# Residue token order, inputs laid out before the launch, four cache places and a two-pass norm in a hybrid attention, convolution and mixture-of-experts layer

## The reference

```python
z = x @ w_in + b_in                      # 5376 columns: q, k, v (12 heads of 64), ua, ub (512 each), two gates (1024 each)
q, k = partial_rotary(q, k, pos)         # first 16 of the 64 dims of a head
# attention: 3 groups of 4 heads, (window, dilation) = (128, 1), (512, 4), (2048, 16);
# query t reads keys t, t-d, t-2d, ...; the groups are merged by softmax over their log-sum-exp
A = attn @ w_attn_out                    # 256 -> 1024
u = ua * sigmoid(ub)
C = silu(LN(causal_depthwise(u, 31 taps))) @ w_conv_out + b_conv_out
h = LN(alpha * x + (sigmoid(gA) * A + sigmoid(gC) * C) @ w_o)
# experts: best of 4 groups, then the 2 best of its 8 SwiGLU experts, gates by softmax
out = LN(alpha * h + moe(h))
```

## Time and profile before

| Engine | busy, us | share of the span |
|---|---|---|
| PE, matmuls | 1188.2 | 92% |
| PE, weight loads | 946.9 | 73% |
| DVE | 842.6 | 65% |
| ACT | 583.2 | 45% |
| POOL | 287.1 | 22% |

### The profile page before, as it was taken

One profiled execution on the slowest core, in us unless ns is written; L12 is line 12 of the kernel. 1 busy time (PEld: TensorE's weight loads), 2 busy tenths in 40 slices (PEclk: granted clock), 3 DMA queues, 4 the chain that ended last, 5 costly groups with the idle time before them and its releaser, 6 DMA issues.

```text
span 1290.2 us, 16384 instructions
## 1 busy us (share of the span) xinstructions
PE 1188.2 (92%) x6098; PEld 946.9 (73%) x6098; DVE 842.6 (65%) x958; ACT 583.2 (45%) x534; POOL 287.1 (22%) x227
## 2 busy tenths in 40 slices
PE   5999999979989999979849999999999999999980
PEld 4899998868878787867536777777777777777760
DVE  1259999611220356444367999888888888888866
ACT  1222221011030224301136877777777777778750
POOL 0144340111012000320021233322333223332110
PEclk8999999978766999988959999999999999999995
DMA  7277733254013042302357999999999999999833
GB/s 224 66 257 278 286 105 111 80 172 153 5 61 119 33 184 109 105 3 100 124 238 285 365 374 368 369 357 357 360 357 363 360 355 364 356 368 367 324 85 141
DMA packets 61201, 293.09 MB, mean 227 GB/s; under 512 B 11492, under 2 KB 36766, under 8 KB 48364
## 3 DMA queue, kind: packets, MB, share of 16 engines
q1 hardware_dynamic: 45149, 262.53, 54.3%
q0 software_dynamic: 12256, 25.98, 6.8%
q10 hardware_dynamic: 3758, 4.06, 1.0%
HBM read 286.83 MB, written 41.12 MB: 254 GB/s over the span
## 4 chain that ended last, share of the span: by engine, by line
PE 87%; DVE 5%; DMA 2%; issue 2%; POOL 1%; ACT 1%; SPq 1%; POOLq 0%; ACTq 0%; DVEq 0%
PE ps L604 10%; PE ps L913 9%; PE ps L915 9%; PE ps L914 9%; PE ps L937 5%; PE ps L939 5%; PE ps L938 5%; PE ps L554 3%; PE ps L556 3%; PE ps L555 3%; PE ps L552 2%; PE ps L755 2%; PE ps L831 2%; PE ps L896 2%; PE ps L799 2%
## 5 line engine op out<-in xcount | busy, mean ns | idle before, releaser
L1623 DVE TENSOR_TENSOR region_b_split<-region_b,z_split 128x2048 fp32r<-128x2048 f32 x96 | 216.9, 2286 | 25.7 <-ACT z_split L1160 25.6
L1623 DVE TENSOR_TENSOR region_a_split<-region_a,z_split 128x2048 fp32r<-128x2048 f32 x96 | 216.7, 2285 | 23.2 <-ACT z_split L1160 23.1
L913 PE MATMUL ps<-z_split,scratch_split 128*96 128x512 f32 x512 | 206.4, 403 | 1.9 <-DVE scratch_split L1628 1.9
L915 PE MATMUL ps<-z_split,scratch_split 128*96 128x512 f32 x512 | 201.8, 394 | 0.0
L1160 ACT CAST z_split<-region_a 128x2048 fp32r<-128x2048 f32 x96 | 179.8, 1908 | 0.0
L1160 ACT CAST z_split<-region_b 128x2048 fp32r<-128x2048 f32 x94 | 176.1, 1908 | 2.0 <-PE ps L915 2.0
L604 PE MATMUL ps<-x_columns,region_b 128*128 128x272 f32 x512 | 149.5, 446 | 7.0 <-DMA region_b<-in_w_in 7.0
L1305 DVE SCALAR_TENSOR_TENSOR z_conv_gates<-scratch,column_vectors,z_conv_gates 128x512 f32<-128x512 f32 (+1 forms) x240 | 133.9, 632 | 0.0
L604 PEld LDWEIGHTS ps<-x_columns,region_b 128*128 128x128 f32 x512 | 107.5, 217 | 30.5 <-DMA region_b<-in_w_in 7.1
L913 PEld LDWEIGHTS ps<-z_split,scratch_split 128*96 128x96 f32 x512 | 85.2, 166 | 33.7 <-DVE scratch_split L1628 2.2
L915 PEld LDWEIGHTS ps<-z_split,scratch_split 128*96 128x96 f32 x512 | 83.1, 162 | 36.5
(11 more groups left out here) (280 smaller groups left out, 1985.4 us busy)
## 6 DMA issues: line engine op xcount, KB each, us to landing
region_b<-in_w_expert_gate SPq DMA_DIRECT2D x16, 2048.0 KB, 14.1
region_a<-in_w_expert_up SPq DMA_DIRECT2D x16, 2048.0 KB, 14.9
region_a<-in_w_expert_gate SPq DMA_DIRECT2D x16, 2048.0 KB, 14.0
region_a<-in_w_expert_down SPq DMA_DIRECT2D x16, 2048.0 KB, 14.6
region_b<-in_w_expert_up SPq DMA_DIRECT2D x16, 2048.0 KB, 15.3
region_b<-in_w_expert_down SPq DMA_DIRECT2D x16, 2048.0 KB, 15.0
region_b<-in_w_in SPq DMA_DIRECT2D x21, 1024.0 KB, 5.3
region_b<-in_cache_kv_w POOLq DMA_DIRECT2D x16, 512.0 KB, 3.9
```

Source lines behind the costliest of these rows:

```text
L913: pe.matmul(out, xh[:, k, :], hi[:, k, :], start=k == 0, stop=False)
L915: last = pe.matmul(out, xl[:, k, :], hi[:, k, :], start=False, stop=k == KD - 1)
L1623: ve.tensor_tensor(low_part[place][:, part], raw[place][:, part], high_part[high or w][:, part].bitcast(F32), ALU.subtract).then_inc(low_s ...
```

## The change

The change has these parts:

1. **Residue order.** The prompt's tokens stand in the order 0, 4, 8, ..., 508, 1, 5, ... in every column tile. The queries and keys of a residue are 128 neighbouring columns. Rotary tables, masks, the rows of x and y are permuted to match. The convolution keeps the order of time: `u` is written back to it (4 DVE instructions in place of 1), and the centring after it returns to residue order (9 in place of 2).
2. **x laid out outside the launch.** x comes as columns, in two halves of 128 lines of 8.5 KB. The 40 transposes and 5 copies go. The low and high parts of x are made in halves. The high parts wait ahead of most of ACT's constant loads.
3. **w_in laid out as pairs**, one line of 8 KB for each partition. Only tiles 0 and 1 are float32 now, tiles 2 and 3 are split.
4. **Small vectors and the convolution's state as columns**, one transfer each; 10 transposes go.
5. **Cached keys and values laid out as tiles**, one transfer of 768 KB for each sequence and kind. The keys come already turned, so the 96 transposes and 16 copies go. Keys and values share four places.
6. **`keys` of the first group** stores 32 partitions x 4 rows: 4 transposes of 32 columns in place of 1 of 128.
7. **Two-pass norm** before the router: DVE subtracts the mean and multiplies by the gain, then multiplies by the inverse root and adds the offset. ACT's pass and the separate scaling go.
8. **Row numbers in place.** Outside POOL's loops, gathers and scatters read `gidx` itself. DVE's first expert splits wait until the first gather is issued.

```diff
-    w_in = a["w_in"][0].rearrange("(k p) n -> p k n", p=P)
+    w_pairs = a["w_in_pairs"]
-    x_p, x_s = a["x_prompt"][0], ...
+    x_p, x_s = a["x_prompt"][0].rearrange("(p r) d -> p r d", r=4), ...
-        kc = eb[:, 6144:9216].rearrange("p (s t c) -> p s t c", s=2, t=6)
-        vc = eb[:, 9216:12288].rearrange("p (s t c) -> p s t c", s=2, t=6)
+        kc = eb[:, 6144:12288].rearrange("p (s t hp k) -> p s t hp k", s=4, t=6, hp=2)
+        vc = eb[:, 6144:12288].rearrange("p (s t c) -> p s t c", s=4, t=6)
...
+            load_x(0)
+            load_pair(0, UA0 // 2)
+            load_x(1)
-            for j in range(4):
+            for j in range(1, 4):
...
-            for n in range(4):
-                if n % 2 == 0:
-                    pe.wait_ge(win_loaded[n // 2], 16)
-                project(n, n // 2, n % 2)
-                if n == 1:
-                    small_turns()
-            pe.wait_ge(x_split, 1)
-            for n in range(4, 8):
+            for h in range(2):
+                pe.wait_ge(x_loaded[h], 16)
+            pe.wait_ge(win_loaded[0], 16)
+            for n in range(2):
+                project(n, 0, n)
+            pe.wait_ge(x_split, 2)
+            for n in range(2, 8):
                 project_split(n, n // 2 % 2, n % 2)
...
-            def cached_keys(b):   # 12 transposes, then cached_scores(b - 1)
+            def cached_keys(b):
+                if b == 0:
+                    pe.wait_ge(qbd_set, 1)
+                pe.wait_ge(cache_loaded[b % 4], 16 * (b // 4 + 1))
...
-                        last = pe.matmul(ps[:, 5, c0:c0 + w], ktr[:, b % 2, tile * 2 + hp, :], q, start=True, stop=True)
+                        last = pe.matmul(ps[:, 5, c0:c0 + w], kc[:, b % 4, tile, hp, :], q, start=True, stop=True)
...
-                    q = zqkv[p0:p0 + 64, Q0 + 2 * g + hp, r:SEQ:4]
+                    q = zqkv[p0:p0 + 64, Q0 + 2 * g + hp, r * P:(r + 1) * P]
...
-                                         zqkv[p0:p0 + 64, K0 + 2 * g + hp, r:SEQ:4], start=True, stop=True)
+                                         zqkv[p0:p0 + 64, K0 + 2 * g + hp, r * P:(r + 1) * P], start=True, stop=True)
...
+            for h in range(2):
+                ac.wait_ge(x_loaded[h], 16)
+                ac.copy(x_hi[:, 4 * h:4 * h + 4, :], xt[:, 4 * h:4 * h + 4, :]).then_inc(x_high, 1)
...
-            ve.tensor_tensor(uext[:, :, PAD:PAD + SEQ], ua[:, :, 0:SEQ], ub[:, :, 0:SEQ], ALU.mult)
+            for c in range(CT):
+                ve.tensor_tensor(uext[:, c, PAD:PAD + SEQ].rearrange("p (q r) -> p r q", r=4), ...)
...
+                by_time = cen[:, :, 0:SEQ].rearrange("p c (r q) -> p c q r", r=4)
+                for half, q0, q1 in ((0, 0, HALF // 4), (1, HALF // 4, P)):
+                    n = 4 * (q1 - q0)
+                    for c in range(CT):
+                        ve.tensor_tensor(by_time[:, c, q0:q1, :], acc[:, c, 4 * q0:4 * q1].rearrange("p (q r) -> p q r", r=4),
+                                         ps[:, 2 + half, 0:n].rearrange("p (q r) -> p q r", r=4), ALU.subtract).then_inc(cen_sb, 1)
...
-                last = ve.tensor_copy(at[rows, :, q:SEQ:4], out_ps[rows, q % 2, hh:HEADS:2, :])
+                last = ve.tensor_copy(at[rows, :, q * P:(q + 1) * P], out_ps[rows, q % 2, hh:HEADS:2, :])
...
+                link(ve.scalar_tensor_tensor(hs, hs, mv[s][0:n, 0:1], g1row[0:n], ALU.subtract, ALU.mult))
                 ve.wait_ge(hsd, t + 1)
-                scaling(s, n, hscale)
-                ve.wait_ge(hnorm, t + 1)
-                link(ve.tensor_tensor(hs, hs, g1row[0:n], ALU.mult))
-                ve.tensor_tensor(hs, hs, b1row[0:n], ALU.add).then_inc(hdone, 1)
+                link(ve.reciprocal(rs[s][0:n], sd[s][0:n]))
+                ve.scalar_tensor_tensor(hs, hs, rs[s][0:n], b1row[0:n], ALU.mult, ALU.add).then_inc(hdone, 1)
...
+            ve.wait_ge(gather_begun, 1)
             split_low("g", 0, 0, GU_PLACE["g"][0])
...
+            def load_cache(i):
+                po.dma_start(eb[:, 6144 + 1536 * (i % 4):6144 + 1536 * (i % 4 + 1)], a["cache_tiles"][i]).then_inc(cache_loaded[i % 4], 16)
             po.wait_ge(tile_mm, 26)
+            for i in range(3):
+                load_cache(i)
             po.wait_ge(rotated, 12)
+            load_cache(3)
+            for i in range(4, 12):
+                po.wait_ge(st_ps, i - 3)
+                load_cache(i)
+            for i in range(12, 16):
+                po.wait_ge(vs_used, i - 11)
+                load_cache(i)
...
+                if value is None:
+                    index = gidx[0:BLK, col]
+                else:
+                    po.tensor_copy(index, gidx[0:BLK, col]).then_inc(copied_sem, 1)
+                    po.wait_ge(copied_sem, value)
```

More of the change, by code:

```diff
@@ L399, in store_rows, with load_x, load_pair @@
                                        skv[t:NS:NT, g].rearrange("p two c -> p (two c)")).then_inc(stored, 16)
-            for s in range(2):
-                sp_e.dma_start(xs[:, 2 * s:2 * s + 2, :], x_p[256 * s:256 * s + 256].rearrange("(t p) d -> p t d", p=P)).then_inc(x_loaded[s], 16)
-            sp_e.dma_start(xs[0:NS, 4, :], x_s).then_inc(x_loaded[1], 16)
-            def load_pair(j, col):
-                sp_e.dma_start(wring[:, j % 2], w_in[:, :, col:col + 256]).then_inc(win_loaded[j % 2], 16)
+            def load_x(h):
+                half = slice(4 * h * N, 4 * (h + 1) * N)
+                sp_e.dma_start(xt_t[:, half], a["x_columns"][:, half]).then_inc(x_loaded[h], 16)
+            def load_pair(j, pair):
+                sp_e.dma_start(wring[:, j % 2].rearrange("p k n -> p (k n)"), w_pairs[pair]).then_inc(win_loaded[j % 2], 16)
             def copy_batch(b):
@@ L754, in cached_values @@
                         o0, w = (b * 8, 8) if g != 1 else (b * 8 + 2 * (tile - 1), 2)
-                        last = pe.matmul(ps[:, 6 + hp, o0:o0 + w], vc[:, b % 2, tile, hp * P:(hp + 1) * P],
+                        last = pe.matmul(ps[:, 6 + hp, o0:o0 + w], vc[:, b % 4, tile, hp * P:(hp + 1) * P],
                                          st_sb[:, g * P + hp * 64 + o0:g * P + hp * 64 + o0 + w],
@@ L1025, in high @@
                 ac.copy(w_hi[:, s, :, tile], wring[:, s, :, tile]).then_inc(w_high, 1)
+            for c in range(2):
+                high(1, c, 16)
             for n in range(8):
@@ L1788, in _ @@
             for s in range(SLOTS):
-                gather(s, slice(s, s + 1), gathered[s], idx_set_e, s + 1)
+                gather(s, slice(s, s + 1), gathered[s], None, None)
+                po.sem_inc(gather_begun, 1)
             def ahead(e, s):
                 po.wait_ge(xgt_ps, e + 1)
-                gather(s, bass.ds(e + 2, 1), gathered[s], idx_set_e, 2 * e + 2 if not isinstance(e, int) or e > 0 else 3)
+                if isinstance(e, int):
+                    gather(s, slice(e + 2, e + 3), gathered[s], None, None)
+                else:
+                    gather(s, bass.ds(e + 2, 1), gathered[s], idx_set_e, 2 * e - 5)
             def back(e, s, value, landed):
@@ L1845, with laid_out @@
            (1, NB, 128, 2, 4, 64), (1, NB, 512, 2, 4, 64), (1, NB, 516, 2, 4, 64), (1, NB, PAD, CC)]
+def laid_out(inputs):
+    by_column = lambda v: np.asarray(v).reshape(-1, P).T
+    x = np.concatenate([inputs["x_prompt"][0].reshape(P, 4, D).transpose(1, 0, 2).reshape(SEQ, D), inputs["x_sample"].reshape(NS, D)])
+    w_in = inputs["w_in"][0].reshape(KD, P, IN_W // 256, 256).transpose(2, 1, 0, 3).reshape(IN_W // 256, P, KD * 256)
+    columns = np.concatenate([by_column(inputs[n][0]) for n in ("b_in", "b_dw", "conv_ln_g", "conv_ln_b", "b_conv_out", "w_dw")], 1)
+    state = inputs["state_conv"][0].reshape(NB, PAD, CT, P).transpose(3, 2, 0, 1).reshape(P, CT * NB * PAD)
+    tiles = []
+    for two in range(2):
+        c = [inputs[n][0][:, :, two].reshape(NB, -1, 2 * P) for n in ("cache_kv_w128", "cache_kv_w512", "cache_kv_w2048")]
+        rows = np.concatenate([c[0][:, None], c[1].reshape(NB, P, 4, 2 * P).transpose(0, 2, 1, 3),
+                               c[2].reshape(NB, -1, 16, 2 * P)[:, :, 0:4].reshape(NB, 1, P, 2 * P)], 1)
+        if two == 0:
+            tiles.append(rows.reshape(NB, 6, P, 2, P).transpose(0, 4, 1, 3, 2).reshape(NB, P, 12 * P))
+        else:
+            tiles.append(rows.transpose(0, 2, 1, 3).reshape(NB, P, 12 * P))
+    tiles = np.concatenate(tiles)
+    return {"cache_tiles": tiles, "x_columns": x.reshape(N, KD, P).transpose(2, 1, 0).reshape(P, KD * N), "w_in_pairs": w_in, "columns": columns, "state_columns": state}
 def kernel(**inputs):
@@ L1853 @@
     arrays, args = {}, {}
-    for name in INPUTS:
+    inputs = {n: np.asarray(v) for n, v in inputs.items()}
+    inputs.update(laid_out(inputs))
+    for name in [*INPUTS, "x_columns", "w_in_pairs", "columns", "state_columns", "cache_tiles"]:
         arrays["in_" + name] = np.ascontiguousarray(inputs[name])
```

244 lines of the change are left out of this document (78 added, 166 removed).

## The result

The changed kernel takes 1245.3 us, the median of four runs (1243.98 to 1247.48), against 1289.26 for the kernel before (1288.73 to 1290.51) on the same chip: a ratio of 0.9664, with a 95% interval of 0.9646 to 0.9683. The forecast was 1249.8. The profiled execution took 1245.54 us with a span of 1243.5, 46.7 less than the span of before; the forecast's sum was 39.6.

What follows compares the result with a forecast made beforehand. PE was taken to bound the kernel, with 87% of the chain that ended last. Savings less two DVE costs summed to 39.6 us, taking the median from 1289.37 to 1249.8 us; range 1239 to 1264.

Steps and rivals of the forecast that it cites:

- Cached keys: Keys stage without transposes: 9.0 us saved, 54 in place of 63, with 14.5 put down to the lower clock.
- The load behind `store_rows`: Load of a w_in pair that PE waits for behind the stores: stall stays, load shrinks, 0.7 us saved.
- First gather: Before the experts: POOL's 4.79 us copy goes and DVE's splits wait behind the gather, 5.0 us saved.
- projection: Four float tiles become two, and small transposes go: 4.0 us saved, the rest keeping its pace.
- Start: First projection matmul at 11.8 in place of 21.82 us, waiting for x and one pair: 10.0 us saved.
- The two strided rewritings on DVE: Writing u in order of time and centring back to residue order: +0.6 and +0.9 us.
- rival C: DVE becomes the bound in both reorderings, at the strided rate: 2.0 and 1.9 us more, 1253.7; chance 10%.
- Attention: Prompt attention with neighbouring columns: the strided weight load's price goes, 0.60 us a step, 9.6 in 16 steps.
- Rival B: In prompt attention, a stride of four floats was already free: 9.6 us less saved, 1259.4; chance 12%.
- A: The clock takes back the saving in the cached keys: 9.0 us less saved, 1258.8; chance 15%.
- D: More than forecast: high clock at start (2), fewer falls between sparser small groups (3), quicker loads (2): 1243 us; chance 10%.
- E: Long 8 KB lines of w_in move slower than 1 KB pieces: 1306 us at 12 us a load; chance 3%.

Runs made afterwards that it cites:

- experiment 3: Changed kernel with two gate quarters, not one, ahead of each sequence of cached values, taken from the first attention steps: 1235.1 us, 0.9578 of the kernel before.
- 4: Changed kernel with the six gate quarters ahead of the key transposes moved to the prompt attention: 1249.9 us, 0.9714 of the kernel before.
- experiment 1: Changed kernel with each sequence's 12 transposes put back right ahead of its 24 score records, results unused: 1256.4 us, 0.9761 of the kernel before.
- 2: Changed kernel with the 12 transposes put back, for six of eight sequences a gate away from the scores: 1257.0 us, 0.9752 of the kernel before.
- 5: Changed kernel without the second half of each sequence's 24 small records in the cached values: 1214.9 us, 0.9434 of the kernel before.
- Experiment 6: Changed kernel with the 20 stores of store_rows issued behind the next w_in pair's load, not ahead of it: 1237.0 us, 0.9592 of the kernel before.
- experiment 7: Changed kernel whose VectorE waits for the second gather's signal, not the first's, before splitting the first expert's weights: 1243.1 us, 0.967 of the kernel before.
- 8: Changed kernel whose prompt attention reads the queries alone 16 bytes apart, keys staying neighbours: 1252.6 us, 0.9744 of the kernel before.
- 9: Changed kernel whose prompt attention reads the keys of the second and third width alone 16 bytes apart: 1253.9 us, 0.9762 of the kernel before.

## Why the prediction was right, and where it was not

The median came out 4.5 us under the forecast and inside its range. Part of that closeness is luck. Three terms were off by 2 us or more: the cached keys gave 10.9 more than forecast, and the load, the gather and the projection took 5.2 of it back. The profiled runs differ by 46.4 us and the medians by 44.0, since the profiled run of before lay 2.6 above its median.

**Cached keys, -9.0 forecast, -19.9 measured.** The step that failed is "the small records are then a larger part of the stretch". The prediction's own numbers say the opposite. Before, 7.9 of transposes, 18.1 of scores and 2 of key transposes are 28 of 50 us at full clock, 56%. After, it is 15.5 + 2 of 39.6, 44%. I compared the groups (one kind of small record less, but scores still between the gates) and not the shares, and so took 14.5 us for the clock where 3.7 came. The table sets the stretches beside each other: the small records' share at full clock in the whole window and in one repeating round (a gate or two, and the small records up to the next), the granted clock of the window, and that behind its slow start, which is one gate in the keys and a whole sequence in the values:

| Stretch | Share, window | Share, one round | Granted clock | Behind the slow start |
|---|---|---|---|---|
| Values, half of the records | 41% | 41% | 0.89 | 1.00 |
| Values, two gates a sequence | 44% | 41% | 0.84 | 0.92 |
| Keys, changed kernel | 44% | 45% | 0.93 | 0.97 |
| Keys, transposes together / apart | 54% | 54% | 0.86 / 0.83 | 0.88 / 0.84 |
| Keys, before | 56% | 54% | 0.80 | 0.82 |
| Keys, one gate for two | 56% | 58 to 62% | 0.68 | 0.70 |
| Values, one gate a sequence | 58% | 58% | 0.62 | 0.63 |

Shares of a round and clocks rank nearly alike, whether the share is moved by gates (3, 4) or by the records themselves (1, 2, 5). It is no exact law: 41% goes with 1.00 and, with groups of 2.58 us in place of 1.27, with two more falls and 0.92, so the length of a group may count as well; no run separates the two there. Of the 19.9 us, 13.1 are the transposes (7.9 of records, 5.2 of clock, by the profile of experiment 1; 15.0 by that of 2), 2.6 the group of scores that now stands ahead of the load, and the last 4.2 (2.3) the tail, where before one more group stood between single gates and went at 4.92; that part is read from the traces and no run isolates it.

**The load behind `store_rows`, -0.7 forecast, +1.7 measured.** That the stall stays was right, though its 9.0 us lie above the 5 to 7 named. That the load shrinks failed here: it took 7.18 beside a cache tile. In the other profiles of the same lists it took 5.28 to 7.48, so the size of this miss is that of one execution. Experiment 6 shows what I did not weigh, that the whole wait was SP's order and could go with one line.

**First gather, -5.0 forecast, -3.0 measured.** The step "DVE's splits wait behind it until about 662" failed: the wait that the change adds is let go when the gather is handed on, not when it is written. With a later signal (experiment 7) the term is -4.8, so the rest of the working held.

**Start, projection, norm, last scatter, cached values, experts** came within 1 us. In the projection there is a fourth wait for POOL's low part (3.5 us in all in place of 2.3), which I did not have. The two strided rewritings on DVE were taken at +0.6 and +0.9 and cost nothing on the path in the trace, so rival C falls. Of the signs named, PE waits for neither `x_lo`, a cast of pair 1 nor a cache tile, and the experts' stage moved by 0.3 us.

**Attention, -9.6 forecast, -9.4 measured,** with half of the reason. I named the weight load as the price; experiments 8 and 9 show that the streamed keys cost as much (7.1 us of the stage alone, for 7.4 of the queries), and that the change had to lay out both. The number came out because I took the new record from another line (L799), whose two sides were both plain. Rival B falls by the same runs. The sentence of the Trainium skill behind it ("SBUF — State Buffer", "Door 1: The DMA port swizzle"), that one can stride 4 fp32 for free, does not hold for PE's reads here: a stride of exactly four floats brings a weight load from 188 to 316 ns and a matmul of 128 columns from 272 to 402. Its other sentence, that each new 16-byte line is paid for, agrees.

**Rivals.** A had the sign of the clock's part wrong, as the forecast did. D named the reason, less clock loss between sparser small groups, but put 3 us on it. E falls: the long lines land in 4.8 us.

## What to carry to other kernels

When records of different weight share a stretch of a busy PE, work out what share of it the small ones have before and after, at full clock, and look for a stretch of the same kernel with that share to read the clock from: work that is moved between stages for nothing else can pay there. The share is a guide and no law, and the stage that hands the work over can lose its cover (6.1 us in experiment 3). Here a record went at the pace of the slower of its weight load and its stream, so the stride had to be taken from both to be gone. A signal that a queue gives on handing a DMA on says nothing of when it is written; if another engine is to keep clear of the gather's work, it needs a later one. A detail of one profile that the timed runs don't repeat, such as a clock's fall, is to be looked for in a second profile of the same lists before it is put down to an edit.

## What the runs showed of the hardware that I had not expected

- PE busy without a gap (57.6 of 57.6 us in the cached values) has a granted clock of 0.62, near its lower level of 0.50, when 24 records of 128x128 weights streamed against 2 to 8 columns stand between two gates. Leaving out half of them gives 29.0 us back where the records alone are worth 10.3.
- Moving the transposes away from the scores, with the same mix, changes nothing: together and a gate apart the kernel takes 1256.4 and 1257.0.
- Where the clock falls differs between executions of the same lists: the cached keys without the idle time take 56.3 us at 0.88 in one profile and 52.8 at 0.94 in another.
- A gather that POOL begins while a DVE subtraction of two SBUF operands runs ends 0.86 to 0.95 us behind that subtraction (3.02, 2.35 and 1.85 us in all against 1.03); a subtraction that begins after it doesn't hold it up.
- A load of 1 MB took 4.88 and 5.03 us before the next cache tile was issued, and 6.25 to 7.48 behind a tile that was issued up to 1.7 us ahead of it.
